# Bias rows written 16 times over and read back by 16 partitions, modulation tiles asked for behind the norm, first feed-forward weights asked for a stage ahead

## The reference

```python
cond = silu(c)
for layer in range(2):
    mod = cond @ w_ada[layer] + b_ada[layer]
    sh1, sc1, g1, sh2, sc2, g2 = split(mod, 6)
    h = rms_norm(x, norm_mix[layer]) * (1 + sc1) + sh1
    y = gated_deltanet(h) if layer == 0 else dilated_attention(h, rel_bias)
    x = x + g1 * y
    h = rms_norm(x, norm_ffn[layer]) * (1 + sc2) + sh2
    gate, up = split(h @ w_ffn_in[layer], 2)          # 1024 -> 2 x 2816
    x = x + g2 * ((silu(gate) * up) @ w_ffn_out[layer])
```

## Time and profile before

| | us |
|---|---|
| median of three timed runs | 4334.72 |
| lowest, highest | 4333.7, 4343.58 |
| the profiled execution's own time | 4341.17 |
| its span | 4338.8 |
| TensorE busy | 4100.5 (95%) |
| VectorE busy | 2088.9 (48%) |
| ScalarE busy | 908.5 (21%) |
| GpSimd busy | 1148.6 (26%) |

### The profile page before, as it was taken

How to read it: one execution, slowest core, us unless ns; L and a number is a source line. 1 busy time by engine, 2 the same in 40 slices (tenths; PEclk the granted TensorE clock), 3 DMA queues, 4 the chain that set the end, 5 groups by cost and what they waited for, 6 DMA issues and landing times. The chain is left out here.

```text
span 4338.8 us, 52254 instructions
## 1 busy us (share of the span) xinstructions
PE 4100.5 (95%) x18989; PEld 2999.2 (69%) x18989; DVE 2088.9 (48%) x3639; ACT 908.5 (21%) x1812; POOL 1148.6 (26%) x894
## 2 busy tenths in 40 slices
PE   7998986999999799999989999999999899999998
PEld 3446955888666478884568844888845688448887
DVE  2666534432343343322466824776224668247752
ACT  2332210000333210001440111222124401112220
POOL 0003302443100044430015500544300154005443
PEclk9998998999999899999999999999999999999999
DMA  6311135333442023335113322233251133222332
GB/s 222 77 39 44 49 85 117 115 89 85 127 127 73 22 80 87 89 86 115 40 39 88 88 68 77 68 87 87 78 117 39 44 86 87 64 77 68 87 89 76
DMA packets 625542, 355.86 MB, mean 82 GB/s; under 512 B 68266, under 2 KB 595403, under 8 KB 625396
## 3 DMA queue, kind: packets, MB, share of 16 engines
q1 hardware_dynamic: 606920, 327.46, 28.1%
q10 hardware_dynamic: 18476, 26.45, 2.3%
HBM read 340.22 MB, written 6.29 MB: 80 GB/s over the span
## 5 line engine op out<-in xcount | busy, mean ns | idle before, releaser
L754 PE MATMUL psum<-h_normed,weight_slot 128*128 128x256 f32 x2816 | 652.2, 385 | 45.9 <-DVE gate L817 26.4
L754 PEld LDWEIGHTS psum<-h_normed,weight_slot 128*128 128x128 f32 x2816 | 544.6, 194 | 128.9 <-DVE gate L817 26.8
L754 PE MATMUL psum<-sums_in,weight_slot 128*128 128x256 f32 x2112 | 486.6, 380 | 9.4 <-DVE sums_in L790 5.0
L754 PEld LDWEIGHTS psum<-sums_in,weight_slot 128*128 128x128 f32 x2112 | 401.9, 191 | 66.1 <-issue 5.7
L722 POOL TENSOR_TENSOR weight_slot<-weight_slot 128x512 f32<-128x512 f32 (+1 forms) x136 | 177.2, 1303 | 925.2 <-DMA weight_slot<-in_w_ffn_in 369.7
L820 DVE COPY work<-psum 128x256 f32<-128x256 f32 x104 | 43.9, 422 | 607.2 <-PE psum L754 607.1
L2927 PE MATMUL psum<-sums_of_h,weight_slot 128*128 128x256 f32 x1280 | 282.8, 379 | 0.0
L2927 PEld LDWEIGHTS psum<-sums_of_h,weight_slot 128*128 128x128 f32 x1280 | 243.2, 190 | 33.1
L3548 DVE SCALAR_TENSOR_TENSOR u<-raw,vectors,u 128x511 f32<-128x511 f32 (+1 forms) x176 | 218.7, 1262 | 93.9 <-ACT u L3527 81.0
L2521 PE MATMUL psum<-h_normed,weight_slot 128*128 128x512 f32 x576 | 255.5, 601 | 1.0 <-ACT raw L2704 1.0
L754 PE MATMUL psum<-sums_hidden,weight_slot 128*128 128x256 f32 x1056 | 243.7, 379 | 0.0
(11 more groups left out here) (471 smaller groups left out, 6143.4 us busy)
## 6 DMA issues: line engine op xcount, KB each, us to landing
weight_slot<-in_w_ffn_in SPq DMA_DIRECT2D x88, 512.0 KB
weight_slot<-in_ffn_w_up SPq DMA_DIRECT2D x88, 512.0 KB
weight_slot<-in_w_gate SPq DMA_DIRECT2D x64, 512.0 KB
weight_slot<-in_w_in SPq DMA_DIRECT2D x40, 512.0 KB, 5.3
weight_slot<-in_dsw_w_in SPq DMA_DIRECT2D x36, 512.0 KB, 7.2
weight_slot<-in_gdn_w_in SPq DMA_DIRECT2D x32, 512.0 KB, 15.8
weight_slot<-in_w_ffn_out SPq DMA_DIRECT2D x64, 256.0 KB
tile_ahead<-in_w_ada SPq DMA_DIRECT2D x16, 1024.0 KB, 6.7
```

The source lines that it names most:

```text
L754: last = nc.tensor.matmul(c.ps[:, 4 * bank + r // 2, (r % 2) * self.HALF:(r % 2 + 1) * self.HALF], c.slots[s][:, b * 512 + k * P:b * 512 + ...
```

## The change

- The scratch has 16 copies of each row in place of 128 (`COPIES`), so each plane's store carries 128 KB. It is read back by eight transfers of 16 partitions for each plane, 32 in all in place of four, each starting its first partition `r` values earlier.
- In ScalarE's program of `swiglu` the first two halves of the modulation tile are asked for behind the norm's shifts. The loads of the table stay ahead of them.
- A new function asks for the weights of a feed-forward's first two steps. It is called in `gdn_core` and in `project_out`, ahead of the output projection's own weights on SyncE and behind a semaphore that GpSimd raises once it has cleared the next stage's semaphores. `swiglu` then runs with `ahead=True`.
- So that both fit in a slot, the weights of the output projections stand at the slot's end.

```diff
@@ class ProjectOut @@
+    @staticmethod
+    def tile(slot, kt):
+        return slot[:, SLOT - kt * P:SLOT].rearrange("p (k n) -> p k n", k=kt)
@@ def project_out(c, layer, w, kt, moving, finish) @@
+        next_cleared = sems[8]
+
+        @block.gpsimd
+        def _(pool):
+            pool.sem_inc(next_cleared, 1)
 
         @block.sync
         def _(sp):
+            sp.wait_ge(next_cleared, 1)
+            first_ffn_weights(c, sp, layer)
             out.sync(sp, 2)
@@
+COPIES = 16
+
+def first_ffn_weights(c, sp, layer):
+
+    for s in range(2):
+        for g in range(2):
+            sp.dma_start(SevenProducts.tile_in(c, s, g), columns(c.ins["w_ffn_in"][layer, :, :], s * (FT // 2) * P + g * F1, P)
+                         ).then_inc(c.next_sems()[(LOAD0, LOAD1)[s]], 16)
@@ class LayerAhead @@
     def clear(self, pool):
         self.c.nc.gpsimd.memset(self.table[BUCKETS:BUCKETS + 1, :], NEG).then_inc(self.cleared, 1)
+        pool.wait_ge(self.cleared, 1)
...
-            act.dma_start(self.scratch[plane, :, :, :], self.rows[:, plane:plane + 1, :].to_broadcast([WH, P, 256])).then_inc(self.rows_stored, 16)
+            act.dma_start(self.scratch[plane, :, :, :], self.rows[:, plane:plane + 1, :].to_broadcast([WH, COPIES, 256])
+                          ).then_inc(self.rows_stored, 16)
@@ def swiglu @@
-                ffn.sync(sp, lambda n0, g: columns(w_in, n0 + g * F1, P), lambda n0, k0, kc: columns(w_out, n0, P)[:, k0:k0 + kc, :])
+                ffn.sync(sp, lambda n0, g: columns(w_in, n0 + g * F1, P), lambda n0, k0, kc: columns(w_out, n0, P)[:, k0:k0 + kc, :],
+                         ahead=True)
...
                     ahead.load_table(act)
+                norm.scalar(act)
+                if ahead is not None:
                     ahead.load_half(act, 0, 0)
                     ahead.load_half(act, 1, 0)
-                norm.scalar(act)
-                if ahead is not None:
                     ahead.keep_rows(act)
@@ def window_attention, SyncE @@
             for j, plane in enumerate((3, 0, 1, 2)):
-                skewed = bass.AP(tensor=scratch.tensor, offset=plane * WH * P * 256 + P - 1, ap=[[255, P], [P * 256, WH], [1, P]])
-                sp.dma_start(biases[:, :, j, :], skewed).then_inc(biases_loaded, 16)
+                for r in range(0, P, COPIES):
+                    skewed = bass.AP(tensor=scratch.tensor, offset=plane * WH * COPIES * 256 + P - 1 - r,
+                                     ap=[[255, COPIES], [COPIES * 256, WH], [1, P]])
+                    sp.dma_start(biases[r:r + COPIES, :, j, :], skewed).then_inc(biases_loaded, 16)
@@ def window_attention, VectorE @@
-            dve.wait_ge(biases_loaded, 64)
+            dve.wait_ge(biases_loaded, 16 * 4 * (P // COPIES))
@@ def build @@
-        scratch = nc.dram_tensor("bias_rows", (4, WH, P, 256), F32, kind="Internal").ap()
+        scratch = nc.dram_tensor("bias_rows", (4, WH, COPIES, 256), F32, kind="Internal").ap()
```

More of the change, by code:

```diff
@@ L590, in __init__ @@
         self.first = before.get("first", 0)
+    @staticmethod
+    def tile(slot, kt):
+        return slot[:, SLOT - kt * P:SLOT].rearrange("p (k n) -> p k n", k=kt)
     def sync(self, sp, ahead=0):
-        stream_weights(sp, self.c, KT, lambda n, slot: [
-            (slot[:, 0:self.kt * P].rearrange("p (k n) -> p k n", k=self.kt), self.load(n))],
+        stream_weights(sp, self.c, KT, lambda n, slot: [(self.tile(slot, self.kt), self.load(n))],
             self.loaded, self.done, self.first, ahead)
@@ L598, in tensor @@
         multiply_steps(pe, self.c, KT, 1, self.loaded, self.done, self.freed, 1, self.kt,
-                       lambda slot, t, k: slot[:, k * P:(k + 1) * P], self.moving, **self.before)
+                       lambda slot, t, k: self.tile(slot, self.kt)[:, k, :], self.moving, **self.before)
     def vector(self, dve, finish, stats):
@@ L616, in scalar, with project_out @@
         stats.root(act)
-def project_out(c, w, kt, moving, finish):
+def project_out(c, layer, w, kt, moving, finish):
     with c.stage(square=[P, 2, S], total=[P, S]) as (block, sems, square, total):
@@ L1421, in gdn_core @@
         consts, t_begun = sems[28:30]
-        half_loaded, (taken, ada_link, ada_summed, ada_biased) = sems[34:36], sems[36:40]
+        half_loaded, (taken, ada_link, ada_summed, ada_biased, next_cleared) = sems[34:36], sems[36:41]
         out = ProjectOut(c, lambda n: columns(c.ins["gdn_w_out"][0, :, :], n * P, P), GH, lambda k: og[:, k, :],
@@ L1625, in _ @@
                             pe.wait_ge(gated, 2 * NCH - 1 + k // HALF)
-                        last = nc.tensor.matmul(c.ps[:, 4 * s, :], c.slots[s][:, k * P:(k + 1) * P], og[:, k, :],
+                        last = nc.tensor.matmul(c.ps[:, 4 * s, :], out.tile(c.slots[s], GH)[:, k, :], og[:, k, :],
                                                 start=(k == 0), stop=(k == GH - 1))
@@ L2310, in first_out_weights @@
     for n in range(2):
-        sp.dma_start(c.slots[n][:, 0:WHG].rearrange("p (k n) -> p k n", k=WHG // P), out_weights(c, n)).then_inc(c.next_sems()[n], 16)
+        sp.dma_start(ProjectOut.tile(c.slots[n], WHG // P), out_weights(c, n)).then_inc(c.next_sems()[n], 16)
 def dilated_attention(c, layer, ahead, scratch):
@@ L2322, in dilated_attention @@
         window_combine(c, o_groups, neg_max, sums, o)
-        project_out(c, c.ins["dsw_w_out"][0, :, :], WHG // P, lambda k: o[:, k, :], add_gated(c, layer, 2))
+        project_out(c, layer, c.ins["dsw_w_out"][0, :, :], WHG // P, lambda k: o[:, k, :], add_gated(c, layer, 2))
 def layer_columns(w, layer, n0, n):
```

## The result

The changed kernel takes 4294.93 us (median of 4 executions, 4291.87 to 4297.74), the kernel before 4339.15 us (median of 4, 4333.7 to 4344.35): ratio 0.9892, 95% interval 0.9877 to 0.9907. The forecast was 4290, its range 4282 to 4305. The profiled execution took 4295.47 us with a span of 4293.7; against the earlier trace rows's kernel (span 4338.8) that is 45.1 us less, where the sum said 44.8. The agreement is better than the steps deserve and in part luck, as the stages show.

| stage | before | after | moved | forecast |
|---|---|---|---|---|
| first feed-forward | 461.5 | 414.9 | -46.6 | -44.3 |
| window attention and its output projection | 453.0 | 451.7 | -1.2 | +1.5 |
| second feed-forward | 418.1 | 414.9 | -3.3 | -2 |
| everything else | 3006.3 | 3012.3 | +6.0 | 0 |

What follows compares the result with a forecast made beforehand. TensorE, busy 95% of the span, was taken as the bound, with one hole in the first feed-forward. Terms summed to -44.8 us, 4341.17 to 4296; 6.5 less for the timed median gave 4290, range 4282 to 4305.

Steps and rivals of the forecast that it cites:

- The stall: First feed-forward: TensorE's waits for gate and weights and its lower-clock groups, behind the bias-row stores, all go; 40.3 us less.
- 75 GB/s for the stores: Bias-row stores from 8 partitions drain at 75 GB/s, so 0.5 MB takes 7 us instead of 55.
- Step 2's weights: First feed-forward: these weights, requested beside modulation tile transfers and stores, come late; 1 us more, bounds 0 and 4.
- First step of layer 0: First feed-forward: weights already in the slot let GpSimd fold from the start; 5 us less, bounds 3 and 6.5.
- First step of layer 1: Second feed-forward: weights fetched ahead shorten the stretch from norm to products; 2 us less.
- Requests ahead in layer 0: Four 512 KB requests before the first output projection's weights, which are used 46 us after their request; cost 0.
- the third weights in layer 1: Second output projection: its third weight request queues behind 2 MB of new requests; 1 us more, bounds 0 and 3.
- The 32 reads: Window attention's start: bias reads on SyncE stand before the second pair's weights; 0.5 us more, bounds 0 and 5.
- A: First feed-forward: a late modulation tile holds VectorE's next combine, 16 us lost, kernel 4306 us; chance 0.12.
- B: Window attention's start: slow small reads on SyncE delay the second pair's weights, at worst 4341 us; chance 0.03.
- C: First feed-forward: the stores' narrow source still holds ScalarE until near 665, kernel say 4325 us; chance 0.05.
- D: First steps of both feed-forwards: clock stays at its upper level, 3 us each, 4284 us; included in the forecast's 0.80.

Runs made afterwards that it cites:

- a1: The kernel before with only 16 copies and the 32 reads; 4306.36 us, ratio 0.9930.
- a4: The changed kernel with 128 copies and four reads again; 4346.2 us, ratio 1.0011.
- b2: The changed kernel with 64 copies (2 MB of stores, eight reads); 4321.86 us, ratio 0.9949.
- b5: The changed kernel with 32 copies (1 MB of stores, 16 reads); 4302.51 us, ratio 0.9912.
- b3: The changed kernel with the modulation tile's first two halves asked for ahead of the norm's scalings again; 4295.56 us, ratio 0.9894.
- b6: The kernel before with 16 copies and the modulation tile's halves behind the norm's scalings, first weights still fetched inside the stage; 4305.32 us, ratio 0.9922.
- b1: The changed kernel with 8 copies and 64 reads of 8 partitions; 4305.76 us, ratio 0.9912.
- c3: The changed kernel with 128 copies and four reads, each plane's store cut into eight pieces issued between steps; 4298.04 us, ratio 0.9896.

## Why the prediction held, point by point

- *The stall, -40.3.* Size right: 40.2 by a1. The size came from step marks, which hold whoever stops TensorE. One part of its explanation was wrong. I followed the releaser of the earlier trace rows, "VectorE's gate", and put 26.45 us on ScalarE's being held by its issues. TensorE waited for the third step's weights, which came slowly beside the stores (a4, b2, b5). The row's own trace that should have warned me is GpSimd's first fold of those weights, 0.23 us ahead of TensorE's matmul at 681.16:

```profile
680.93 1.26 POOL L722 TENSOR_TENSOR weight_slot<-weight_slot 128x512 f32<-128x512 f32 x1 [41.88 <-DMA weight_slot<-in_w_ffn_in]
```

  The forecast didn't suffer, because 16 copies take away both chains; a cure for ScalarE alone (the stores issued by an idle engine) would by my reading have given 26 us, and the weights would still have been late. That version was not tried.
- *75 GB/s for the stores.* Wrong by half, 51. At 0.5 MB it makes 10 us instead of 7, and both hide. At 4 MB it makes 82 us instead of 55: in the kernel before ScalarE had issued its last store by 675.23, but the stores still moved 0.20 MB from 704 to 708, and the fourth step's weights were late too. It would have mattered at 1 MB.
- *Step 2's weights, +1.* Not seen: the step's weights were in time, no wait.
- *First step of layer 0, -5, bounds 3 and 6.5.* 6.4 from a1 to the changed kernel, near its upper bound: norm to P4 came to 13.11 us instead of the 14.37 of the earlier trace rows. That fits the head start on the folds, for which I allowed up to 2 us; no run takes the head start away alone. b3 and b6 put the 6.4 us on the weights and not on the order.
- *First step of layer 1, -2.* 3.3 by the stage, 2.4 by norm to P4.
- *Requests ahead in layer 0, 0; the third weights in layer 1, +1.* No wait in the one, 0.38 us in the other.
- *The 32 reads, +0.5.* 0: 16.34 us for all, as by the shortest of the earlier trace rows (16.2) rather than by the median (18.9), and no wait for the second pair's weights. By the port rule of the Trainium skill ("SBUF — State Buffer", section "Door 1: The DMA port swizzle") it would have been 1 us dearer, an estimate from its 104 GB/s; it didn't show. The reads moved 0.55 MB in the 4 us from 1042 to 1046, 138 GB/s, with one read behind another to other partitions; I had put 150.
- *Rivals.* A: the longest tile transfer took 9.7 us to land, and nothing waited for one. B: needs dearer issues than there are; b1 shows its onset at 64 reads. C: fell, 0.68 us an issue. D: fell. In both feed-forwards the first products still ran at the lower level (a granted clock of 0.50 from 622 to 626 and from 1486 to 1490); it is at 1.00 from 628 and from 1494 on.
- *The sum.* 6.3 us too small in the stages that changed (2.3 + 2.7 + 1.3), and made good by 6.0 us of drift in the others; that the two cancelled was luck. The 6.5 us that I took off for the difference between the profiled execution and the median had no such footing: the median of before, with one run more, was 4339.15, 4.4 us above the one shown. Without that subtraction the forecast would have been 4296, 1 us off.

## What to carry to other kernels

Where an engine stops behind a long narrow transfer, look at each queue by itself: a rate for all of them is not the rate of one, and a trace's releaser is the last event, not always the needed one. Check it against the data that the stopped instruction reads, and ask which step would stop next if this one didn't. A small backlog in the same place (0.5 MB) cost nothing here, so cutting the transfer into pieces between steps was nearly as good as making it smaller (2 us dearer, c3).

## What the hardware showed that I had not expected

- A store from 8 partitions moved 51 GB/s at 0.42 of the DMA engines' time, and this rate stayed the same with weights beside it. The weights beside it were slower by far: 1.05 MB in the 28 us from 652 to 680 in the kernel before, 1.1 MB in 4 us in b5 once the stores were gone.
- Such a backlog holds also the issues of another queue: SyncE's four took 0.37, 4.56, 10.80 and 8.92 us in b2, and 0.37 to 0.75 us each in the changed kernel.
- One read of 64 KB into 16 partitions cost SyncE 0.51 us of its time, one of 32 KB into 8 partitions 0.37 us.
- VectorE's and GpSimd's additions slow each other: 2.1 to 2.3 us for 128x1024 on VectorE and 2.13 for 128x512 on GpSimd together, 1.22 and 1.27 apart. The rows look like turns rather than a lower rate: in the changed kernel (from 626 on) a fold ends at 627.45, a sum at 628.54, a fold at 629.66, a sum at 630.74, each 1.1 us behind the other engine's, about the time of one alone. No run here tests this further.
